# More products of a constant on TensorE in a two-layer attention and expert trunk

## The reference, cut to what matters

```python
u = modulate(rmsnorm(h, norm_mix[layer]), sh_m, sc_m)      # "mix0", "mix1"
h = h + g_m[:, None, :] * mix
u = modulate(rmsnorm(h, norm_ffn[layer]), sh_f, sc_f)      # "ffn0", "ffn1"
h = h + g_f[:, None, :] * moe_ffn(u, w_router[layer], ...)
# nsa: o = gates[..., 0:1] * o_cmp + gates[..., 1:2] * o_sel + gates[..., 2:3] * o_win
# moe_ffn: scores = sigmoid(u @ w_router); top 8 of 64 experts of each token
#          sum of their SwiGLU outputs by normed scores, and a shared expert
```

## Time and profile before

| | us |
|---|---|
| three runs | 1396.72, 1393.27, 1393.61 (median 1393.61) |
| the profiled execution | 1396.53 |
| its span, first to last instruction | 1394.8 |
| mean granted TensorE clock | 0.991 of 2.4 GHz |
| TensorE matmuls busy | 1338.6 (96%) |
| DVE, ACT busy | 428.8, 268.4 |
| HBM, mean over the span | 367 GB/s |

### The profile page before, as it was taken

The page is one execution under the profiler, slowest core; times in us unless marked ns, Lnnn a source line. Parts: engine busy times, 40 slices in busy tenths (PEclk is TensorE's granted clock), DMA queues, the critical chain, the costliest instruction groups (busy, mean ns, idle before and its releaser), DMA issues.

```text
span 1394.8 us, 20069 instructions
## 1 busy us (share of the span) xinstructions
PE 1338.6 (96%) x8011; PEld 783.8 (56%) x8011; DVE 428.8 (31%) x969; ACT 268.4 (19%) x534; POOL 32.1 (2%) x82
## 2 busy tenths in 40 slices
PE   5998989999999999999899899899999999999997
PEld 1887865465444444444388788754564444444442
DVE  1799672101111111111183698611111111111111
ACT  2222531110111111011133563410110111111100
POOL 4000000001000000000000000000010000000000
PEclk9999999999999999999999999999999999999999
DMA  9999666999999999999999602579999999999996
GB/s 381 390 421 421 266 247 260 385 421 361 423 420 421 422 421 421 421 421 421 421 417 420 252 1 90 220 307 383 420 362 422 420 421 422 421 421 422 420 421 286
DMA packets 71774, 512.94 MB, mean 368 GB/s; under 512 B 8240, under 2 KB 8448, under 8 KB 9728
## 3 DMA queue, kind: packets, MB, share of 16 engines
q1 hardware_dynamic: 70560, 509.64, 88.6%
q0 software_dynamic: 832, 1.39, 0.5%
q10 hardware_dynamic: 288, 0.61, 0.1%
HBM read 510.55 MB, written 1.05 MB: 367 GB/s over the span
## 4 chain that ended last, share of the span: by engine, by line
PE 80%; DMA 8%; DVE 7%; ACT 2%; issue 2%; SPq 1%; DVEq 0%; ACTq 0%
PE PS L987 24%; PE PS L977 13%; PE PS L995 12%; PE PS L1011 11%; PE PS L565 6%; DMA ring<-in_w_in_a_units 4%; DMA ring<-in_w_exp 4%; DVE ring L614 2%; PE PS L737 2%; PE PS L1023 2%; SPq L1397 1%; PE PS L692 1%; PE PS L1852 1%; PE PS L1032 1%; PE PS L716 1%
## 5 line engine op out<-in xcount | busy, mean ns | idle before, releaser
L987 PE MATMUL PS<-ring,scratch 128*32 128x512 f32 (+2 forms) x2176 | 353.7, 593 | 6.7 <-DMA ring<-in_w_exp 5.3
L987 PEld LDWEIGHTS PS<-ring,scratch 128*32 128x32 f32 (+2 forms) x2176 | 111.0, 122 | 242.3 <-issue 240.6
L1342 DVE TENSOR_TENSOR scratch<-PS,gate_row 128x512 f32<-128x512 f32 x100 | 69.2, 692 | 462.3 <-PE PS L995 462.3
L977 PEld LDWEIGHTS PS<-scratch,u 128*128 128x128 f32 x1600 | 186.2, 194 | 38.4 <-issue 36.5
L977 PE MATMUL PS<-scratch,u 128*128 128x128 f32 x1600 | 195.4, 281 | 1.4 <-ACT scratch L1206 1.4
L995 PE MATMUL PS<-ring,scratch 128*32 128x512 f32 (+2 forms) x1088 | 182.2, 596 | 3.4 <-DMA ring<-in_w_exp 2.2
L1011 PE MATMUL PS<-scratch 128*128 128x512 f32 x384 | 172.7, 592 | 0.0
L565 PE MATMUL PS<-ring,uT 128*128 128x256 f32 x672 | 148.6, 380 | 3.6 <-DMA ring<-in_w_in_a_units 3.4
L1214 ACT ACTIVATE scratch<-PS 128x256 f32<-128x256 f32 x50 | 19.2, 384 | 672.9 <-PE PS L987 672.9
L565 PEld LDWEIGHTS PS<-ring,uT 128*128 128x128 f32 x672 | 126.3, 190 | 22.6 <-issue 4.2
L1330 DVE TENSOR_TENSOR scratch<-scratch,PS 128x256 f32<-128x256 f32 x50 | 21.1, 422 | 329.7 <-ACT scratch L1214 329.7
(11 more groups left out here) (346 smaller groups left out, 856.9 us busy)
## 6 DMA issues: line engine op xcount, KB each, us to landing
ring<-in_w_exp SPq DMA_DIRECT2D x384, 1024.0 KB, 16.4
ring<-in_w_ada_columns SPq DMA_DIRECT2D x48, 1024.0 KB, 25.6
ring<-in_w_in_a_units SPq DMA_DIRECT2D x12, 1024.0 KB, 27.5
ring<-in_w_ada_units SPq DMA_DIRECT2D x8, 1024.0 KB, 16.1
ring<-in_w_cmp_units SPq DMA_DIRECT2D x8, 1024.0 KB, 24.0
ring<-in_w_sh_units SPq DMA_DIRECT2D x6, 1024.0 KB, 13.7
ring<-in_w_kv_b_units SPq DMA_DIRECT2D x6, 1024.0 KB, 22.4
ring<-in_w_o_a_units SPq DMA_DIRECT2D x4, 1024.0 KB, 26.4
```

Source lines behind the costliest of these rows:

```text
L977: mm = pe_.matmul(PS[:, bank, i * w:(i + 1) * w], u[:, t, k * P:(k + 1) * P], hot[:, t, :], start=(t == 0), stop=(t == NT - 1))
L987: mm = pe_.matmul(PS[places, GU, :], x[:, kk, places], gate_and_up, start=(kk == 0), stop=(kk == KC - 1))
L1342: dve.tensor_tensor(y_rows[:, half * 512:(half + 1) * 512], PS[:, Y0 + half, :], gate_row[:, half * 512:(half + 1) * 512], ALU.mult).then_ ...
```

## The change

Layer 0's heads get 8, 3, 6, 3, 3 and 3 products of 124 columns ahead of batches 0 to 5. In ffn0, mix1 and ffn1 two products of 512 columns stand between tile 0 and tile 1 of the normed rows. Ten of 512 columns stand ahead of the wait for the mask in each layer, and three ahead of the wait for the head gates. Layer 1's heads keep theirs.

```diff
--- before.py
+++ after.py
@@ -726,8 +726,8 @@
                     pe_.wait_ge(heads_read, b0 + b - 1)
                 elif banks_free and banks_free[b]:
                     pe_.wait_ge(*banks_free[b])
-                if kind == "nsa" and b in BUSY_BEFORE_HEADS:
-                    pe_keep_busy(pe_, BUSY_BEFORE_HEADS[b], heads_bank(kind, b), slice(4 * (DH + 1), 512 - P))
+                if b in BUSY_BEFORE_HEADS[kind]:
+                    pe_keep_busy(pe_, BUSY_BEFORE_HEADS[kind][b], heads_bank(kind, b), slice(4 * (DH + 1), 512 - P))
                 for i in range(4):
                     if i * (t + 1) % 4 == 0:
                         pe_.wait_ge(probsT_ready, banks_up_to(kind, b) + i * (t + 1) // 4 + 1)
@@ -748,7 +748,7 @@
                 turn(b)
             weigh(len(batches) - 1)
 
-        BUSY_BEFORE_HEADS = {0: 1, 1: 1, 2: 1, 3: 1, 4: 4}
+        BUSY_BEFORE_HEADS = {"fox": {0: 8, 1: 3, 2: 6, 3: 3, 4: 3, 5: 3}, "nsa": {0: 1, 1: 1, 2: 1, 3: 1, 4: 4}}
         CMP_TURNED_AT = 6
         cmp_raw = ada_parts
         cmp_logits = PS[:, 6, 512 - NT * H * NB:512].rearrange("p (t h n) -> p t h n", t=NT, h=H)
@@ -882,6 +882,8 @@
             if tag in BUSY_BEFORE_NORMED:
                 pe_keep_busy(pe_, *BUSY_BEFORE_NORMED[tag])
             for t in range(NT):
+                if t and tag in BUSY_BEFORE_NORMED:
+                    pe_keep_busy(pe_, 2, BUSY_BEFORE_NORMED[tag][1])
                 pe_.wait_ge(rows_normed, NT * NORMED.index(tag) + t + 1)
                 for k in range(KC):
                     if t == 1 and k == KC // 2:
@@ -1057,6 +1059,7 @@
             pe_sum_tiles_to_rows(pe_, of_halves[:, :], router_ps).then_inc(routing["router_turned"], 1)
             pe_gate(pe_, 2 * layer + 1)
 
+            pe_keep_busy(pe_, 10, Y0 + 1)
             pe_.wait_ge(routing["mask_ready"], layer + 1)
             pe_.matmul(ranks_ps[:, 0, :], before[:, :], routed[:, 0, :], start=True, stop=True).then_inc(m["more_added"], 1)
             pe_.matmul(ranks_ps[:, 1, :], ones[:, :], routed[:, 0, :], start=True, stop=False)
@@ -1792,6 +1795,7 @@
             def pick_cmp_logits(b):
                 if b == 0:
                     pe_.wait_ge(sem("cmp_raw_copied"), 1)
+                    pe_keep_busy(pe_, 3, 4)
                     pe_.wait_ge(sem("gates_ready"), 1)
                     for t in range(NT):
                         for q in range(2):
```

## The result

The changed kernel takes 1410.26 us (median of 4 runs, 1409.07 to 1415.11), the kernel before on the same chip 1393.44 us (4 runs). The ratio is 1.0123, 95% interval 1.0108 to 1.0139: slower by 1.2%, which is small but clear of the noise. The profiled execution took 1409.07 us.

A forecast was written before the change was run, and what follows sets the result against it. TensorE bounds, with layer 0's expert DMAs pinned to it until about 340 us. 3.1 + 3.1 + 4.8 - 0.8 + 0 + 1.1 + 1.4 + 0.4 = +13.1 us gave 1409.6, median 1408, range 1401 to 1414.

The forecast's parts named there:

- A product's price: On TensorE, a product of 512 columns costs 0.86 us at full clock, one of 124 columns 0.23 us.
- Layer 0's heads: 26 narrow products ahead of layer 0's head batches cost +4.8 us, bounds +2.4 and +7.1.
- Only the wait at the place hides a product: A product hides only where TensorE waits at that place: 0.87 us before batch 0, 0.34 before batch 5.
- The clock's return: Behind each layer's mask wait, full clock gives back 2.6 us against ranks 5.7 us late: net +3.1 us.
- The estimate of a third for the small matmuls: Behind the mask, 1.2 us of the other 4 us of half clock come back on small matmuls and transposes.
- No stage gives the delay back: A microsecond lost ahead of the experts is lost at their end, in both layers; no later stage catches up.
- The rival that the ring swallows layer 0's delay: DMA rate sets the expert stage from its start, so layer 0's delay vanishes: 1402.5 or 1401 us; chance 9%.
- Between the normed tiles: Two wide products between the two normed tiles cost 0 in ffn0, +1.1 us in mix1, +1.4 us in ffn1.
- The head gates: Three wide products ahead of layer 1's head gates cost +0.4 us, bounds -1.5 and +3.1.
- The turning at 160 us: At the transposes of layer 0's normed heads, the half-clock stretch may go: -0.8 us, half of 1.6.
- The rival that the products fit: Wide products take 0.22 us, so ten end within the mask's wait: 1391.4 us, not slower; chance 3%.
- The allowance for the median: The median lies 2.9 us below the profiled execution; half of that was taken off 1409.6, giving 1408 us.

The follow-up runs named there:

- early group: The kernel before with ten wide products at the head of expert group 1 of layer 0; ratio 1.0093.
- late group: The kernel before with ten wide products at the head of expert group 18 of layer 0; ratio 1.0037.
- mask runs: The kernel before with only the ten wide products ahead of the mask in both layers; 1403.66 us, ratio 1.0071.

## Why the prediction was right

The forecast was 1408 us with 92% on slower; 1410.26 was measured. Its steps, by the account and the runs above:

- **A product's price.** 0.86 and 0.23 us were forecast from the earlier trace rows. The step from ten to twenty gives 0.858. The narrow ones take 0.235 to 0.257, but delay the next batch by 0.22 each, since the heads' matmuls behind them are 0.10 us shorter.
- **Layer 0's heads** cost 4.46 us against +4.8. The eight ahead of batch 0 cost 1.1 us where I had 0.97, the three ahead of batch 5 at most 0.1 where I had 0.35.
- **Only the wait at the place hides a product.** Shown in both directions: three ahead of the mask move nothing, ten move the ranks by 5.9 us.
- **The clock's return was capped.** 2.80 and 2.77 us against 2.6 forecast, and three products win the same. The estimate of a third for the small matmuls was slightly low.
- **No stage gives the delay back.** The early group shows it. The rival that the ring swallows layer 0's delay fell with it; the late group shows what truth it had, 3.8 us of slack, taken up by a delay from beyond the last standstill.
- **Between the normed tiles** ffn1 cost 1.6 us against +1.4: the 0.3 us that I took back at the router's DMA wait came again as a wait for the modulation.
- **The head gates** came out at nothing, against +0.4. The products started VectorE's step 0.5 us later, and the wait of 0.48 us that it had behind was gone with the half clock. That VectorE sets the pace from its step on held to 0.02 us. That the clock would not fall there held in all three executions with these products.
- **The turning at 160 us.** I counted half of 1.6 us, since the edit doesn't fill the wait. The trace shows the whole, 1.63. But six of the nine kernels without this edit show it too (1.80 us from L474 to the output product in the early, late and mask runs), so the runs can't credit the edit with it: in the profiled execution of before, as in two others, the clock happened to fall there.
- **The rival that the products fit** is out: a wide product takes 0.86 us. The Trainium skill (TensorE: Matmul & The Clock Gate, Back-to-back issue gap) gives, as an estimate from its formula, 0.22 us for a matmul of 512 columns; these traces have two records of 0.43 us each. The expert stage's records of the same width (128x64 by 128x512) do run 0.22 us apart; why the two kinds differ is not shown.
- **The allowance for the median.** The sum gave 1409.6 for the profiled execution, which took 1409.07. I took 1408 for the median, which was 1410.26, so halving the 2.9 us was the wrong way. The new kernel's other runs are up to 6 us longer than its profiled one, at mean clocks of 0.994 to 0.996 against 0.998.
- **What was luck.** The terms of the products themselves were not: heads, tiles and masks come to 13.5 us in the forecast (4.8 + 0 + 1.1 + 1.4 + 3.1 + 3.1) and to 13.5 in the traces (4.46 + 0.09 + 1.11 + 1.61 + 3.08 + 3.12). The rest is chance of the two executions compared, by where the clock was low in each: -1.6 us at the turning and 0 at the head gates, where I had -0.8 and +0.4, and +0.75 elsewhere, mostly by two new half-clock stretches in the expert stages, where I had nothing.

## What to carry to other kernels

Products that only keep TensorE busy were free here up to the length of the wait in front of which they stand, counted in their own measured price, and cost one for one beyond it; three fitted and ten did not. What they can win is bounded by the half-clock stretch behind the wait, which is read from the granted clock before anything is added. In this kernel a delay ahead of the last standstill of the prefetching DMAs arrived whole, and one behind it arrived less the time that TensorE still waited for weights. Read an edit's cost between two instructions right round it: a stage that begins earlier can give that back as a wait ahead of the edit.

## What the runs showed of the hardware

The half-clock stretches are not a property of the kernel alone. Behind a mask's wait of 2.7 us with no product in it the clock fell in all twelve cases, for 3.4 us twice, 6.8 us nine times and 17 us once. At the head gates, after 2.4 us of wait, it fell in eight of nine executions without products there, and in none of the four with one or three. Behind the wait of 0.8 us ahead of the turning of layer 0's heads it fell in three of nine. Behind the last long waits for weights of a layer, about 2.5 to 3 us, it fell for 3.4 us in some executions and not in others.

The same code of layer 1's attention, from the gates' matmuls to the output product, took 56.8 to 56.9 us in executions without a stretch, 58.3 to 58.4 with one of 6.8 us, 63.29 with one of 13.7 us, and 64.77 with two of 10.2 us. One execution stayed at half clock for 17 us from a wait of 2.7 us on, through the routing and the first expert matmuls, with TensorE busy. The spread between runs of one kernel goes with this: the 28 runs of the kernel before on one of the chips reach from 1391.39 us at a mean clock of 0.996 to 1404.83 us at 0.985. It is a reason to read such an edit stage by stage and not from single times.
